# Memory keys and values computed first, and the convolution's tap products moved to ScalarE, in a one-core decoder layer

## What is computed

```python
x = x + 0.5 * swiglu_1(rmsnorm(x))                # width 1024 -> 2816 -> 1024
q, k, v, a, g = split(rmsnorm(x) @ w_in)          # five times 512 columns
o_a = dilated_window_attention(q, k, v)           # 8 heads; samples use a cache of 2048 rows
u = a * sigmoid(g)                                # 512 channels
y = causal_depthwise_conv(u, conv_w) + conv_b     # 31 taps
o_b = silu(layernorm(y))
x = x + concat(o_a, o_b) @ w_out
mk, mv = rmsnorm(mem) @ w_ck, rmsnorm(mem) @ w_cv # 256 memory tokens
x = x + cross_attention(rmsnorm(x) @ w_cq, mk, mv) @ w_co   # samples use cached keys, values
x = x + 0.5 * swiglu_2(rmsnorm(x))
y = rmsnorm(x)
```

## Time and profile before

| | us |
|---|---|
| median of 3 runs | 2943.33 (2942.31 to 2949.12) |
| the profiled execution | 2947.46 |
| its span in the trace | 2945.7 |
| TensorE matmuls busy | 2704.1 (92%) |
| VectorE busy | 1144.0 (39%) |
| GpSimd busy | 704.8 (24%) |
| ScalarE busy | 539.1 (18%) |

### The profile page before, as it was taken

How to read it: one execution, slowest core, us unless ns; L and a number is a source line. 1 busy time by engine, 2 the same in 40 slices (tenths; PEclk the granted TensorE clock), 3 DMA queues, 4 the chain that set the end, 5 groups by cost and what they waited for, 6 DMA issues and landing times.

```text
span 2945.7 us, 44667 instructions
## 1 busy us (share of the span) xinstructions
PE 2704.1 (92%) x16941; PEld 2506.7 (85%) x16941; DVE 1144.0 (39%) x2097; ACT 539.1 (18%) x1185; POOL 704.8 (24%) x391
## 2 busy tenths in 40 slices
PE   6999999999989995878887988879899999999998
PEld 4999999999979994756546888739799999999997
DVE  6322222222257997423333131612522322223224
ACT  3100100000022111455221122311300001000013
POOL 2222222223313341322000210102233332222210
PEclk8999999999999997989898999999999999999999
DMA  4111111111101222344983111642111111111101
GB/s 126 38 49 43 43 43 43 43 43 43 43 29 35 67 89 66 117 154 150 270 236 122 43 45 73 219 178 77 36 43 43 44 49 43 49 43 43 43 14 61
DMA packets 214544, 223.54 MB, mean 76 GB/s; under 512 B 11450, under 2 KB 181494, under 8 KB 210387
## 3 DMA queue, kind: packets, MB, share of 16 engines
q1 hardware_dynamic: 197479, 194.54, 21.7%
q10 hardware_dynamic: 17004, 28.21, 2.6%
HBM read 190.05 MB, written 32.67 MB: 76 GB/s over the span
## 4 chain that ended last, share of the span: by engine, by line
PE 73%; issue 10%; DVE 8%; DMA 4%; ACT 2%; DVEq 1%; PEld 1%; SPq 1%; POOL 0%; ACTq 0%; PEldq 0%; POOLq 0%
PE ps L602 20%; PE ps L604 20%; PE ps L603 20%; PE ps L611 1%; DVE ya L1552 1%; PE ps L924 1%; DMA Kw<-in_cache_win_k 1%; PE ps L809 1%; PE ps L1031 1%; PE ps L820 1%; PE ps L880 1%; DVE hidl L1449 1%; DVE rs L1427 1%; PE ps L894 1%; DVE hl L1416 1%
## 5 line engine op out<-in xcount | busy, mean ns | idle before, releaser
L602 PE MATMUL ps<-hh,wh 128*128 128x384 f32 (+1 forms) x2688 | 882.6, 328 | 48.5 <-DVE hl L1481 29.2
L604 PE MATMUL ps<-hl,wh 128*128 128x384 f32 (+1 forms) x2688 | 881.2, 328 | 0.0
L603 PE MATMUL ps<-hh,wl 128*128 128x384 f32 (+1 forms) x2688 | 881.2, 328 | 0.0
L602 PEld LDWEIGHTS ps<-hh,wh 128*128 128x128 f32 x2688 | 508.7, 189 | 51.1 <-issue 49.9
L547 POOL CAST wh<-raw 128x1024 fp32r<-128x1024 f32 x136 | 148.5, 1092 | 1550.0 <-PE ps L604 1393.8
L603 PEld LDWEIGHTS ps<-hh,wl 128*128 128x128 f32 x2688 | 508.7, 189 | 0.0
L604 PEld LDWEIGHTS ps<-hl,wh 128*128 128x128 f32 x2688 | 508.5, 189 | 0.0
L1461 DVE TENSOR_TENSOR ht<-ps,sg 128x384 f32<-128x384 f32 x132 | 70.7, 535 | 898.9 <-PE ps L604 896.2
L549 POOL TENSOR_TENSOR wl<-raw,wh 128x1024 fp32r<-128x1024 f32 x148 | 381.7, 2580 | 93.5 <-ACT wh L1203 82.6
L602 PE MATMUL ps<-hidh,bh 128*128 128x384 f32 (+1 forms) x1056 | 346.6, 328 | 11.7 <-DVE x L1473 11.7
L1473 DVE SCALAR_TENSOR_TENSOR x<-ps,x 128x384 f32<-128x384 f32 (+1 forms) x528 | 276.4, 533 | 185.4 <-PE ps L604 185.1
(11 more groups left out here) (214 smaller groups left out, 2774.0 us busy)
## 6 DMA issues: line engine op xcount, KB each, us to landing
raw<-in_ffn_gate SPq DMA_DIRECT2D x44, 512.0 KB, 3.8
raw<-in_ffn_up SPq DMA_DIRECT2D x44, 512.0 KB, 3.8
raw<-in_ffn_down SPq DMA_DIRECT2D x44, 512.0 KB, 3.2
Kw<-in_cache_win_k SPq DMA_DIRECT2D x48, 256.0 KB, 7.1
Vw<-in_cache_win_v SPq DMA_DIRECT2D x48, 256.0 KB
raw<-in_w_in SPq DMA_DIRECT2D x20, 512.0 KB, 3.8
Kw<-in_cache_win_k SPq DMA_DIRECT2D x8, 1024.0 KB, 12.6
Vw<-in_cache_win_v SPq DMA_DIRECT2D x8, 1024.0 KB
```

The costliest lines, as they stand in the source:

```text
L602: pe.matmul(out, w_hi_, a_hi, start=first, stop=False)
L603: pe.matmul(out, w_lo_, a_hi, start=False, stop=False)
L604: return pe.matmul(out, w_hi_, a_lo, start=False, stop=last)
```

## The change

- Stage 1 now computes the memory's keys and values as well: `plan` begins with `w_ck`, `w_cv`, and SyncE loads the two memory tiles first, then x tiles and weight units in turn. The norms of memory and of x are taken by token before the turn (ACT `Square` with an accumulated sum). The memory tiles are scaled before the turn; for x the inverse root is spread over the partitions by a matmul of ones with a diagonal matrix, and the first norm is done in the same stage. Stage 2 begins with SwiGLU 1.
- Stage 3: ACT multiplies each tap (`product`) between its copies, under a schedule of 2.4 products for each chunk of `w_in`; two `prod` buffers; DVE adds. `Us` is laid out token-major, and a channel tile's 64 sample columns take one multiplication of 31 x 64, one reduction and one bias addition.
- Stage 4 is the convolution's layer norm alone. SyncE issues the loads of stage 5 after barrier 3 instead of 4; POOL sorts q and k then, and v after barrier 4.
- The samples' cross-attention keeps keys of four samples; scores alternate between two samples, values between four.
- `hh`, `hl` serve `w_in` too; other buffers move.

```diff
-    plan = [("ffn1", 6 * FG), ("w_in", 20), ("w_ck", 8), ("w_cv", 8), ("w_out", 8), ("w_cq", 8), ("w_co", 8),
+    plan = [("w_ck", 8), ("w_cv", 8), ("ffn1", 6 * FG), ("w_in", 20), ("w_out", 8), ("w_cq", 8), ("w_co", 8),
             ("ffn2", 6 * FG)]
...
+        def load_tile(m):
+            if m >= 3:
+                sp.wait_ge(Z["ssq"], m - 2)
+                if m - 3 < MT:
+                    sp.wait_ge(Z["mt"], 1)
+                else:
+                    sp.wait_ge(L["xin_free"], L.base["xin_free"] + 2 * (m - 3 - MT + 1))
+            n, t = tile_rows(m), m - MT
+            src = mem_tok[m * P:m * P + n, :] if m < MT else x_tok[t * P:t * P + n, :] if t < QT else xs_tok
+            sp.dma_start(xin[0:n, m % 3, :], src).then_inc(L[f"in{m % 3}"], 16)
+
+        def load_kv(u):
+            load_unit(u % 2, u + 1, W[("w_ck", "w_cv")[u // 8]][:, :, u % 8 * P:(u % 8 + 1) * P])
+
+        for m in range(MT):
+            load_tile(m)
...
         for t in range(QT + 1):
...
+            load_tile(MT + t)
+            load_kv(t)
         sp.dma_start(cc_in[:], cache_conv).then_inc(S["conv"]["cc_in"], 16)
+        for u in range(QT + 1, 16):
+            load_kv(u)
         ffn_loads("ffn1")
         in_loads()
-        first_loads("w_ck")
-
+
+        A = S["pa"]
         sp.wait_ge(phase_end, 3 * 3)
-        sp.dma_start(min_[:], mem_tok).then_inc(S["mem"]["in"], 16)
-        col_loads("w_ck", SLOTS)
-        col_loads("w_cv")
-
-        A = S["pa"]
-        sp.wait_ge(phase_end, 3 * 4)
...
+                        if p == 0 and dst is vc:
+                            pool.wait_ge(phase_end, 3 * 4)
...
+        mem_turn()
         for t in range(QT + 1):
...
+            x_turn(t)
+            if t >= 1:
+                spread(t - 1)
+            kv_unit(t)
+        spread(QT)
...
+        kv_unit(QT + 1)
+        kv_tokens(0)
+        for u in range(QT + 2, 16):
+            kv_unit(u)
+        kv_tokens(1)
         barrier(pe, 1)
-        norm(S["n1"], CHUNKS, sq)
         ffn("ffn1", S["n1"])
...
+            def product(k, t):
+                act.wait_ge(C["glu"], 2 * k + 2)
+                j = k * (CONVW - 1) + t - 1
+                if j >= 2:
+                    act.wait_ge(C["tap"], k * CONVW + t - 1 if t > 2 else k * CONVW - 2 + t)
+                act.activation(prod[:, j % 2, :], U[:, k, t:t + SEQ], ACT.Copy, scale=taps[:, k, t:t + 1]
+                               ).then_inc(V["prod"], 1)
+
+            made = 0
+            for w in range(5 * CT):
+                for c in range(NC):
+                    slot = w * NC + c
...
+                    if w < 2 * CT:
+                        gate_unit(w, c, slot % 4)
+                    else:
+                        stored_unit(w - 2 * CT, c, slot % 4)
+                    due = max(0, (slot - 2 * NC + 1) * 12 // 5)
+                    while made < min(due, len(todo)):
+                        product(*todo[made])
+                        made += 1
...
+            if 4 <= u < 12:
+                act.wait_ge(raw_full[u % 2], 16 * ((u + 4) // 2 + 1))
+                act.wait_ge(w_hi, u + 4)
+                act.copy(wh[:, u % 4], raw[:, u % 2]).then_inc(w_hi, 1)
...
+        def sample_conv(k):
+            row = Us[:, k, 0:TS, :]
+            windows = bass.AP(row.tensor, row.offset, [list(row.ap[0]), [NB, CONVW], [1, TSAMP]])
+            weights = taps[:, k, :].unsqueeze(2).to_broadcast([P, CONVW, TSAMP])
+            if k >= 1:
+                dve.wait_ge(V["res"], V.base["res"] + 4 + 2 * k)
+            dve.tensor_tensor(tapped, windows, weights, ALU.mult).then_inc(V["t"], 1)
+            dve.wait_ge(V["t"], V.base["t"] + k + 1)
+            dve.tensor_reduce(ya[:, k, SEQ:T], tapped.rearrange("p t n -> p n t"), AX.X, ALU.add).then_inc(V["res"], 1)
+            dve.wait_ge(V["res"], V.base["res"] + 4 + 2 * k + 1)
+            dve.tensor_scalar(ya[:, k, SEQ:T], ya[:, k, SEQ:T], vecs[:, V_CB + k:V_CB + k + 1], None, ALU.add
+                              ).then_inc(V["res"], 1)
+
+        gated(0)
+        for k in range(CT):
+            dve.wait_ge(C["glu"], 2 * k + 2)
+            dve.tensor_scalar(ya[:, k, 0:SEQ], U[:, k, 0:SEQ], taps[:, k, 0:1], vecs[:, V_CB + k:V_CB + k + 1],
+                              ALU.mult, ALU.add).then_inc(C["tap"], 1)
+            for t in range(1, CONVW):
+                j = k * (CONVW - 1) + t - 1
+                dve.wait_ge(V["prod"], V.base["prod"] + 2 + j + 1)
+                dve.wait_ge(C["tap"], k * CONVW + t)
+                dve.tensor_tensor(ya[:, k, 0:SEQ], ya[:, k, 0:SEQ], prod[:, j % 2, :], ALU.add).then_inc(C["tap"], 1)
+            if k + 1 < CT:
+                gated(k + 1)
+            sample_conv(k)
         barrier(dve, 3)
...
                 for k in range(KT):
-                    mm = pe.matmul(ps[32 * b:32 * b + 32, 2, 0:NMEM], cqc[:, b, k, :], cKT[:, b % 2, k, :],
-                                   start=(k == 0), stop=(k == KT - 1))
-                mm.then_inc(Y["s_full"], 1)
+                    for b in (b0, b0 + 1):
+                        mm = pe.matmul(ps[32 * b:32 * b + 32, 2, 0:NMEM], cqc[:, b, k, :], cKT[:, b, k, :],
+                                       start=(k == 0), stop=(k == KT - 1))
+                mm.then_inc(Y["s_full"], 2)
+
+            for b in range(3):
+                turn_keys(b)
+            pair_scores(0)
+            turn_keys(3)
+            pair_scores(2)
...
-            for b in range(4):
-                for half in range(2):
-                    for j in range(2):
+            for half in range(2):
+                for j in range(2):
+                    for b in range(4):
                         mm = pe.matmul(ps[32 * b:32 * b + 32, 4 + half, :], cPT[:, j, 32 * b:32 * b + 32],
```

More of the change, by code:

```diff
@@ new lines, in kv_tokens @@
+        def kv_tokens(j):
+            if j == 1:
+                act.wait_ge(M["kvst"], 16)
+            for g_ in range(4):
+                t, h = divmod(g_, 2)
+                act.wait_ge(M["tok_t"], 4 * j + g_ + 1)
+                act.copy(kvtok[:, t, 512 * h:512 * h + 512], ps[:, 4 + g_ % 2, :]).then_inc(M["tok"], 1)
+            act.wait_ge(M["tok"], 4 * j + 4)
+            act.dma_start(mem_o["kv"[j]], kvtok[:]).then_inc(M["kvst"], 16)
+        for m in range(MT):
+            squares(m)
@@ new lines, in _ @@
+        for m in range(MT):
+            root(m)
+        act.wait_ge(L["vecs"], L.base["vecs"] + 2)
+        act.wait_ge(Z["mt"], 1)
+        for k in range(KT):
+            act.activation(mh[:, k, :], ps[:, k // 2, k % 2 * NMEM:(k % 2 + 1) * NMEM], ACT.Copy,
+                           scale=vecs[:, G_MEM + k:G_MEM + k + 1]).then_inc(Z["mhi"], 1)
+        for t in range(QT + 1):
+            squares(MT + t)
+            root(MT + t)
+            for j in tile_work(t):
+                x_hi(j)
+            if t >= 1:
+                kv_out(t - 1)
@@ L1165, in _ @@
+        rest = list(range(2 * KT, 3 * KT))
+        for u in range(QT, 16):
+            for j in rest[:2]:
+                x_hi(j)
+            rest = rest[2:]
+            kv_out(u)
+            if u == QT + 1:
+                kv_tokens(0)
+        kv_tokens(1)
         barrier(act, 1)
-        norm(S["n1"], CHUNKS, x, sq, rs, tb, hh)
         ffn("ffn1", S["n1"])
+        act.wait_ge(M["mkst"], 16)
+        act.wait_ge(M["kvst"], 32)
         barrier(act, 2)
-        norm(S["nm"], CHUNKS, x, sq3, rs3, tb3, h3h)
@@ L1273, in _ @@
             exp(0, 1)
-            for kind in "fvk":
+            for kind in "vkf":
                 for half in range(2):
```

476 lines of the change are left out of this document (256 added, 220 removed).

## The result

The changed kernel took 2922.1 us (median of 6 runs, 2910.2 to 2929.0) against 2946.7 for the kernel before beside it: a ratio of 0.9909, 95% interval 0.9890 to 0.9927. In a second series it was 0.9891 (0.9869 to 0.9914). It is about 1% faster, 27 and 32 us by these two ratios; the forecast was 62.5 us, and 2922 lies outside its range of 2851 to 2906.

The account below looks back on a forecast made before the run. VectorE was taken to bound stage 3, where TensorE idled 24 us at the end, and the change's worth to lie in the edges around SwiGLU. 26 - 4 - 55 - 11.5 - 18 = -62.5 gave 2881 from 2943.3, range 2851 to 2906.

Parts of the forecast that it names:

- Stage 1: Start to first SwiGLU product: taking in keys and values moves it from 63.7 to 92; +26 us, bounds +15 and +36.
- the norm of x is hidden: Stage 1: VectorE's work for this norm, about 40 us of the 90, is covered by other work.
- Rival (d): Stage 1 is held up more, each first load taking 7.1 us; +10 us, 2891; chance 0.10.
- Stage 3: Convolution: VectorE stays the bound at 1.25 us a tap; -4 us, bounds -24 and +15.
- Rival (b): Stage 3: copies absorbed, reduction not strided in effect, TensorE ends the stage; -20 us, 2861; chance 0.13.
- rival (e): Stage 3: product and addition don't overlap, 2.35 us a tap, slower than before; 132 us more, 3013; chance 0.04.
- Rival (a): Stage 3: ScalarE's copies and handovers don't hide, a tap costs 1.40 us; +18 us, 2899; chance 0.16.
- Stage 4: Between barriers 3 and 4: 49.7 us left against 104.6; -55 us, -60 to -47.
- Start of stage 5: Behind barrier 4: first scores after 2.8 us instead of 15.4; -11.5 us, -13 to -9.
- The loads and two sorts are done: Start of stage 5: both are finished by then, so scores wait only for 8 transposes and two copies, 2.8 us.
- Cross-attention: Samples' part: alternating scores and values overlap, values 4.9 us instead of 10.34; -18 us, 0 to -22.
- Rival (c): Samples' cross-attention: alternating groups bring nothing; +18 us, 2899; chance 0.08.

Follow-up runs that it names:

- e13: Changed kernel with the edits of e2 and e3, and 16 of 24 tiles of normed x moved behind the last copy of x; 2905.0 us, ratio 0.9842.
- e2: Changed kernel with the w_cv units' rounded halves made on GpSimd instead of ScalarE; 2916.4 us, ratio 0.9881.
- e3: Changed kernel with the keys' token turns put behind unit 13 instead of unit 9, on TensorE and ScalarE; 2911.3 us, ratio 0.9881.
- e4: Changed kernel with the prompt's taps fused again on VectorE and no products for them on ScalarE; 2913.3 us, ratio 0.9854.
- e9: Changed kernel with fused prompt taps in two alternating sums on VectorE and the samples' products on ScalarE; 2903.0 us, ratio 0.9826.
- e1: Changed kernel with the window attention's two starting credits given after barrier 3 instead of barrier 4; 2906.0 us, ratio 0.9861.
- e10: Changed kernel with the window attention's loop written out twice in TensorE's stream alone; 2912.6 us, ratio 0.9853.
- e5: Changed kernel with samples' cross-attention scores one slot after the other and the values' loops swapped, two of one group in a row; 2927.5 us, ratio 0.9917.
- e12: Changed kernel with the edits of e2 and e3 together; 2915.1 us, ratio 0.9849.

## Why the prediction was right or wrong

**Stage 1, wrong (+45.9 - 2.3 instead of +26).** The step that failed is the sentence that the norm of x is hidden, its VectorE work being 40 of 90 us. I compared sums and not the order. TensorE does unit t behind the turn of x's tile t; the turn waits for VectorE's copy of tile t-1; the copy stands behind three tiles of x, each with a wait for ScalarE and a subtraction that GpSimd holds up. I priced a step by its loads, (5.6 + 3.4)/2 = 4.5. The copies of x stood 9.3 us apart at step 6 and 7.1 at steps 7 and 8, and the token turns put 7.25 more idle in front of the last units. e13 shows the cause, with 100.0 for units about 4 us apart, as far as one run can that has e2's and e3's edits as well. What separates that from the forecast's 92 I have not tried. Its trace says where it lies: the last of the 16 splits ended at 88.7 instead of 81.6, with a step of 9.3 us in front of unit 8, and the rest behind it was 11.3 for 10.4. Rival (d) gave the stage 10 us more for another reason, the loads. They did not set the period: in e2 the splits were 4 us apart with the same loads. The 2 us given back to SwiGLU 1 came (795.3 to 793.0).

**Stage 3, right in size (-6.6 for -4), wrong in its inside.** The prediction's own terms give 1149.5 - 1151.8 = -2.3, which it put as -4. Splits 14 as counted (18 before), reduction 3.67 for 3.7, sample part 6.14 for 6.1, addition 1.225 for 1.22. The handover between dependent instructions was 0.105 us and not 0.03, just past my bound of 0.1. What I didn't see is what the step is worth: I took the fused tap of the prompt for what was left of 1.47 without asking what it would be alone. It is 1.32 (e4), so the product on ScalarE buys nothing. The gain against before is that of the sample part. I wrote that TensorE would wait "within the time that VectorE needs anyway": TensorE ended at 284.2 us and VectorE at about 285, so this held by 1 us; ScalarE's place had become a second bound. Rival (b), with TensorE at 268, is what e9 makes true; rival (e) falls with 1.33 a tap. Rival (a), 1.40, can't be put aside: with the late products the mean step is 1.375, where the forecast's 1.25 and 8 us for copies come to 1.32. The term came out near its size because the other error had the opposite sign: the 120 additions, GpSimd's stops among them, took 192.5 us for 150 + 8 + 41 = 199. That is luck and not understanding.

The reduction's size was also put beside the Trainium skill, "Vector Engine (DVE) Microarchitecture Reference", SBUF access granule: by it 3.4 to 5.0, the traces give 3.46 to 3.80, its lower end.

**Stage 4, right (-55.8 for -55).** The store took 7.45 for 7.0. The first column sums took 9.45 at a granted clock of 0.80; the sum of 49.7 has the 10 that was given for the lower clock, not the 7.5.

**Start of stage 5, wrong (-2.4 for -11.5).** The step: "The loads and two sorts are done". I had moved the SyncE instructions in my mind, but not what they wait for. Their first pass needs a credit that TensorE and VectorE give at the head of their own stage 5 code, behind barrier 4. e1 gives it earlier and gets the missing 9.9 us.

**Scores to the mix loads, +12.4 not foreseen.** 6.9 us is one jump, shown in the trace and removed in e10; the rest lies within the scatter of this stretch, as the second profiles of both kernels show.

**Cross-attention, right (-16.2 for -18).** A pair of scores 3.65 to 4.7 for 3.6, values 5.3 for 4.9. By "TensorEngine Tiling (Array Packing)" of the Trainium skill, Tiling Modes, the values would take an estimated 3.5. The traces agree: at a granted clock of 1.00 they took 3.64 us (3.68 in e5). The 4.9 was near the 5.34 of the changed kernel's two passes for a reason that the prediction doesn't have: they ran at a clock of 0.68, which cost 1.7 us each. Rival (c) falls with e5's scores.

The direction was right; the range failed because three misses had one sign. Two are places where I took work to be covered, the norm of x in stage 1 and the early loads of stage 5; the third is a jump that nobody forecast, and scatter.

## What to carry to other kernels

When work is moved beside other work, don't compare sums of busy time: write down for one period who waits for whom in each engine's fixed order, and look for the small operation (here a copy of 1.3 us) that stands behind a long helper. When a load is moved ahead of a barrier, follow every semaphore that it waits for to the instruction that raises it, starting credits too. Before splitting a fused instruction in two, measure what the fused one costs alone: by columns a multiply-add costs what an addition costs, and independent neighbours, which hide the handover, bring more than the split.

## What the runs showed of the hardware that I had not expected

- A jump back to a loop's head took 5.7 to 6.9 us in ten profiles and 0.2 in e13, whose TensorE stream is that of e12 (5.9); written out, the loop runs without it.
- A fused multiply-add and an addition over 1024 columns take 1.284 and 1.225 us, and start 1.32 and 1.33 us apart when each waits for the last; independent fused ones start 1.196 apart. So the handover costs about 0.12 us.
- GpSimd's subtraction stretched VectorE's subtractions of tiles to up to 2.4 us, but none of the products that read a PSUM bank. In the changed kernel, stage 1 (ns min/median/max, first and last start):

```profile
L1654 DVE SCALAR_TENSOR_TENSOR tb<-x,vecs,ps x24: 530/601/609, 33.9 to 90.4; 128x384 f32<-128x384 f32 x16, 128x320 f32<-128x320 f32 x8
```
```profile
L1643 DVE TENSOR_TENSOR hl<-tb,hh x24: 479/550/2447, 35.0 to 94.6; 128x384 fp32r<-128x384 f32 x16, 128x320 fp32r<-128x320 f32 x8
```

- Products of 32 stationary columns overlap with those of the next column group if at most two of one group follow each other, and hardly after longer runs. At a granted clock of 1.00, 32 records of 512 columns took 3.64 us with one of a group in a row, 3.68 with two (e5) and 8.86 with four (before); 32 of 256 columns took 3.65 with one and 6.23 with eight (scores in e5).
- The same 32 records took 5.34 us at a granted clock of 0.68 and 3.64 at 1.00: before an order is judged by such a row, its clock has to be read.
